# Block 1's expert weights read in whole rows, with the order of the gate and up products changed to fit

## The reference, cut to what matters

```
hidden = silu(x @ w_gate[e]) * (x @ w_up[e])
y      = hidden @ w_down[e]
lat[tokens of e] += g2 * affinity * y
```

## Time and profile before

| what | value |
|---|---|
| time, median of 3 runs | 2313.15 us (2310.91 to 2315.34) |
| the profiled execution's own time | 2319.69 us |
| its span | 2318.0 us |
| TensorE matmuls busy | 2019.3 us, 87% |
| DVE busy | 1720.3 us, 74% |
| ACT busy | 1246.9 us, 54% |
| mean rate of the DMA engines | 275 GB/s |

### The profile page before, as it was taken

The page is one execution under the profiler, slowest core; times in us unless marked ns, Lnnn a source line. Parts: engine busy times, 40 slices in busy tenths (PEclk is TensorE's granted clock), DMA queues, the critical chain, the costliest instruction groups (busy, mean ns, idle before and its releaser), DMA issues.

```text
span 2318.0 us, 30942 instructions
## 1 busy us (share of the span) xinstructions
PE 2019.3 (87%) x9479; PEld 1669.3 (72%) x9479; DVE 1720.3 (74%) x1894; ACT 1246.9 (54%) x1464; POOL 309.1 (13%) x313
## 2 busy tenths in 40 slices
PE   3999999837999999999598888944999999999980
PEld 2888878636888877877476777843888888888760
DVE  5676665398999999998534544443999999999877
ACT  2311112206888878777524412213888888888763
POOL 1000001100100011110301540113010001000023
PEclk9999999858999999999798999966999999999995
DMA  9276863607999999999711113344999999999986
GB/s 314 81 248 223 265 217 110 244 10 276 382 380 388 382 379 389 383 380 349 276 38 55 31 36 117 118 172 141 400 412 411 411 412 412 411 411 412 377 312 231
DMA packets 241520, 637.19 MB, mean 275 GB/s; under 512 B 20340, under 2 KB 57480, under 8 KB 241452
## 3 DMA queue, kind: packets, MB, share of 16 engines
q1 hardware_dynamic: 209536, 524.35, 60.3%
q0 software_dynamic: 27680, 97.70, 12.0%
q10 hardware_dynamic: 4236, 14.27, 1.6%
HBM read 575.83 MB, written 60.41 MB: 274 GB/s over the span
## 4 chain that ended last, share of the span: by engine, by line
PE 65%; DVE 12%; DMA 9%; issue 5%; SPq 4%; ACT 3%; POOL 1%; ACTq 0%; DVEq 0%; POOLq 0%; PEldq 0%
PE ps L1962 19%; PE ps L1963 19%; PE ps L1965 19%; DMA ring<-in_moe_w_down 5%; SPq L522 4%; PE ps L2370 1%; DVE mL L1469 1%; DMA h_dram<-h2t 1%; DMA ring<-in_ada_w 1%; PE ps L2085 1%; DVE top_i L1452 1%; DVE top_v L1451 1%; DVE affT L1454 1%; DVE xz L1615 1%; PE ps L2220 1%
## 5 line engine op out<-in xcount | busy, mean ns | idle before, releaser
L1839 DVE TENSOR_TENSOR mL<-ring,mH 128x1024 fp32r<-128x1024 f32 x384 | 454.7, 1221 | 37.8 <-ACT mH L1166 34.0
L1469 DVE TENSOR_TENSOR mL<-ring,mH 128x1024 fp32r<-128x1024 f32 x384 | 455.4, 1221 | 31.7 <-ACT mH L994 22.4
L994 ACT ACTIVATE mH<-ring 128x1024 fp32r<-128x1024 f32 x384 | 401.6, 1062 | 97.7 <-PE ps L1965 62.8
L1962 PE MATMUL ps<-mH,xsH 128*128 128x512 f32 x1088 | 437.4, 402 | 7.4 <-DVE mL L1839 4.4
L1965 PE MATMUL ps<-mH,xsL 128*128 128x512 f32 x1088 | 426.9, 392 | 0.0
L1963 PE MATMUL ps<-mL,xsH 128*128 128x512 f32 x1088 | 426.7, 392 | 0.0
L1166 ACT ACTIVATE mH<-ring 128x1024 fp32r<-128x1024 f32 x384 | 390.9, 1054 | 31.9 <-PE ps L1965 31.9
L1962 PEld LDWEIGHTS ps<-mH,xsH 128*128 128x128 f32 x1088 | 205.9, 189 | 48.8 <-issue 7.3
L1965 PEld LDWEIGHTS ps<-mH,xsL 128*128 128x128 f32 x1088 | 205.6, 189 | 45.2
L1963 PEld LDWEIGHTS ps<-mL,xsH 128*128 128x128 f32 x1088 | 206.0, 189 | 39.6
L1962 PE MATMUL ps<-mH,hidH 128*128 128x512 f32 x544 | 216.8, 399 | 13.0 <-DVE hidL L1514 5.8
(11 more groups left out here) (402 smaller groups left out, 3030.9 us busy)
## 6 DMA issues: line engine op xcount, KB each, us to landing
ring<-in_w_expert_gate SPq DMA_DIRECT2D x144, 512.0 KB
ring<-in_w_expert_up SPq DMA_DIRECT2D x144, 512.0 KB
ring<-in_w_expert_down SPq DMA_DIRECT2D x144, 512.0 KB
ring<-in_moe_w_gate SPq DMA_DIRECT2D x128, 512.0 KB
ring<-in_moe_w_up SPq DMA_DIRECT2D x128, 512.0 KB
ring<-in_moe_w_down SPq DMA_DIRECT2D x128, 512.0 KB
ring<-in_ada_w SPq DMA_DIRECT2D x96, 512.0 KB
yslot_dram<-xz POOLq DMA_DIRECT2D x31, 512.0 KB, 7.0
```

Source lines behind the costliest of these rows:

```text
L994: act.activation(mH[:, m % WSETS, :], ring[:, m % RING, :], ACT.Copy).then_inc(S["m1_hi"], 1)
L1469: dve.tensor_tensor(mL[:, m % WSETS, :], ring[:, m % RING, :], mH[:, m % WSETS, :].bitcast(F32), ALU.subtract).then_inc(S["m1_lo"], 1)
L1839: dve.tensor_tensor(mL[:, wset, :], ring[:, slot, :], mH[:, wset, :].bitcast(F32), ALU.subtract).then_inc(S["m2_lo"], 1)
L1962: pe.matmul(o, high, rh, start=start, stop=False)
```

## The change

Chunks 0 to 7 become gate, 8 to 15 up, each one k with all 1024 columns, as down already was. TensorE multiplies each chunk for both halves of the columns, except the last three of up (LATE = 3): chunks 13, 14 and 15 are first multiplied for the first half, then `m1_up_half` is raised, and then for the second half, each raising `m1_used` as it ends. ACT takes one SiLU of both halves at m = 13. DVE multiplies half 0 at m = 19 and half 1 at m = 20; ACT copies the transposed halves at m = 21 and 22, DVE subtracts at m = 20 and 22. TensorE makes all transposes behind chunk 15: first half, next expert's tokens, second half.

```diff
@@ -19,6 +19,7 @@
 RING = 12
 SPLIT_RING = 6
 ADA_RING = 4
+LATE = 3
 WSETS = 6
 E1 = 16
 CAP1 = 2 * T // E1
@@ -30,7 +31,7 @@
     h2_done x1_done var2 rstd2 h2_out y_ready zs_hi tr2 h2T_ready sq2 zs_lo
     rt_done wait_passed ada_done split_done z_done m1_lo hy_done pool_out unused_zero m2_y final_done consts
     masks var_ready rstd_ready stored m1_tok m1_y_done zero_row tok_zero rows_zero rows_in small_in
-    silu_ready sq_done mod_ready tr_ready tr_hi split_hi f_part cv_done c_copied route1 e1_exp m1_used m1_hi
+    silu_ready sq_done mod_ready tr_ready tr_hi split_hi f_part cv_done c_copied route1 e1_exp m1_used m1_up_half m1_hi
     m1_xT m1_xT_hi slots_ready m1_silu m1_hT m1_hT_hi if_zero gate_in if_hi v_even gate_exp branch d2_out uc_ready 
     q_mm pm_ready pv hn_tr num_out final_in dve_steps cols_tr mod_mm xn_done
     tr_lo sums_out sums2_out sums_in row_cols row_tr row_copied rows_out rows_here c_here mid_tr tr_mid v_mm pool_steps neg_out mb_in mask_done exp_done small_ready small_exp sq_out intra_out kt_mm kw_out st_mm c_ready hd_out cell_w ov_l last_y last_out row_one aff_ready affT_tr m1_xT_lo m1_hid m1_hT_lo if_lo v_odd if_mm pool_mm k_mm k_out s_mm
@@ -255,7 +256,7 @@
         [("m1_xT", 2 * E1), ("m2_xT", 2 * (E2 + 1 + NOVF))],
         [("m1_xT_hi", 2 * E1), ("m2_xT_hi", 2 * (E2 + 1 + NOVF))],
         [("m1_xT_lo", 2 * E1), ("m2_xT_lo", 2 * (E2 + 1 + NOVF))],
-        [("m1_silu", 2 * E1), ("m2_silu", E2), ("ov_silu", NOVF)],
+        [("m1_silu", E1), ("m2_silu", E2), ("ov_silu", NOVF)],
         [("m1_hid", 2 * E1), ("m2_hid", E2), ("ov_hid", 2 * NOVF)],
         [("m1_hT", 2 * E1), ("m2_hT", E2), ("ov_hT", 2 * NOVF)],
         [("m1_hT_hi", 2 * E1), ("m2_hT_hi", E2), ("ov_h", 2 * NOVF)],
@@ -513,13 +514,7 @@
                     sp.wait_ge(S["m1_lo"], 24 * e + c - RING + 1)
                     if not static(q):
                         settle(sp)
-                if c < 16:
-                    n, kp = c // 8, (c % 8) // 2
-                    src = (moe_g, moe_u)[c % 2][e, :, 2 * kp:2 * kp + 2, 512 * n:512 * n + 512]
-                    dst = ring[:, s, :].rearrange("p (k n) -> p k n", k=2)
-                else:
-                    src, dst = moe_d[e, :, c - 16, :], ring[:, s, :]
-                sp.dma_start(dst, src).then_inc(ring_in[s], 16)
+                sp.dma_start(ring[:, s, :], (moe_g, moe_u, moe_d)[c // 8][e, :, c % 8, :]).then_inc(ring_in[s], 16)
 
         in_pairs(sp, E1, m1_step)
 
@@ -1006,12 +1001,12 @@
         def m1_step(q, r):
             e = 2 * q + r
             for m in range(24):
-                if m == 13 or m == 21:
-                    n = m // 21
-                    act.wait_ge(S["m1_used"], 24 * e + 8 * n + 8)
-                    act.activation(sg[:, 512 * n:512 * n + 512], ps[:, n, :], ACT.Silu).then_inc(S["m1_silu"], 1)
-                if m == 19 or m == 23:
-                    j = m // 23
+                if m == 13:
+                    act.wait_ge(S["m1_used"], 24 * e + 8)
+                    act.activation(sg.rearrange("p (a b) -> p a b", a=2), ps[:, 0:2, :],
+                                   ACT.Silu).then_inc(S["m1_silu"], 1)
+                if m == 21 or m == 22:
+                    j = m - 21
                     act.wait_ge(S["m1_hT"], 2 * e + j + 1)
                     act.activation(hidH[:, 4 * j:4 * j + 4, :].rearrange("p a b -> p (a b)"), ps[:, 2 * j, :],
                                    ACT.Copy).then_inc(S["m1_hT_hi"], 1)
@@ -1502,13 +1497,17 @@
                     tokens(e + 1, 1 - r, 0)
                 if m == 6 and not (static(q) and e == 0):
                     y_out(q, 0) if r == 1 else y_out(q - 1, 1)
-                if m == 13 or m == 21:
-                    n = m // 21
-                    dve.wait_ge(S["m1_silu"], 2 * e + n + 1)
+                if m == 19 or m == 20:
+                    n = m - 19
+                    if n == 0:
+                        dve.wait_ge(S["m1_silu"], e + 1)
+                        dve.wait_ge(S["m1_up_half"], e + 1)
+                    else:
+                        dve.wait_ge(S["m1_used"], 24 * e + 16)
                     dve.tensor_tensor(hid[:, 512 * n:512 * n + 512], sg[:, 512 * n:512 * n + 512], ps[:, 2 + n, :],
                                       ALU.mult).then_inc(S["m1_hid"], 1)
-                if m == 19 or m == 23:
-                    j = m // 23
+                if m == 20 or m == 22:
+                    j = m // 22
                     dve.wait_ge(S["m1_hT_hi"], 2 * e + j + 1)
                     part = hidH[:, 4 * j:4 * j + 4, :].rearrange("p a b -> p (a b)")
                     dve.tensor_tensor(hidL[:, 4 * j:4 * j + 4, :].rearrange("p a b -> p (a b)"), ps[:, 2 * j, :],
@@ -2129,20 +2128,29 @@
             e = 2 * q + r
             first = static(q) and e == 0
             pe.wait_ge(S["m1_xT_lo"], 2 * e + 2)
+
+            def rows_part(m, halves):
+                k, w = m % 8, [slice(512 * n, 512 * n + 512) for n in halves]
+                return three([ps[:, 2 * (m // 8) + n, :] for n in halves], xsH[:, r, k, :], xsL[:, r, k, :],
+                             [(mH[:, m % WSETS, at], mL[:, m % WSETS, at]) for at in w], k == 0, k == KD - 1)
+
             for m in range(24):
-                pe.wait_ge(S["m1_lo"], 24 * e + m + 1)
                 if m < 16:
-                    n, kp, u = m // 8, (m % 8) // 2, m % 2
-                    bank = ps[:, n + 2 * u, :]
-                    if m % 8 == 0 and not first:
-                        pe.wait_ge(S["m1_hid"], 2 * e + n - 1)
+                    if m == 0 and not first:
+                        pe.wait_ge(S["m1_hid"], 2 * e)
                         pe.wait_ge(S["m1_hT_lo"], 2 * e)
-                    for k2 in range(2):
-                        k = 2 * kp + k2
-                        w = slice(512 * k2, 512 * k2 + 512)
-                        last = three([bank], xsH[:, r, k, :], xsL[:, r, k, :],
-                                     [(mH[:, m % WSETS, w], mL[:, m % WSETS, w])], k == 0, k == KD - 1)
+                    if m < 16 - LATE:
+                        pe.wait_ge(S["m1_lo"], 24 * e + m + 1)
+                        last = rows_part(m, (0, 1))
+                    else:
+                        if m == 16 - LATE:
+                            for m0 in range(m, 16):
+                                pe.wait_ge(S["m1_lo"], 24 * e + m0 + 1)
+                                last = rows_part(m0, (0,))
+                            last.then_inc(S["m1_up_half"], 1)
+                        last = rows_part(m, (1,))
                 else:
+                    pe.wait_ge(S["m1_lo"], 24 * e + m + 1)
                     k = m - 16
                     if k == 0 and not first:
                         pe.wait_ge(S["m1_y_done"], e)
@@ -2152,12 +2160,10 @@
                                  [(mH[:, m % WSETS, 512 * n:512 * n + 512], mL[:, m % WSETS, 512 * n:512 * n + 512])
                                   for n in range(2)], k == 0, k == KD - 1)
                 last.then_inc(S["m1_used"], 1)
-                if m == 13:
+                if m == 15:
                     h_transposes(e, 0)
-                if m == 15:
                     if not (static(q) and e == E1 - 1):
                         x_transposes(e + 1, 1 - r, 16 * q + (16 if r == 0 else 32))
-                if m == 17:
                     h_transposes(e, 1)
 
         in_pairs(pe, E1, m1_step)
```

## The result

The changed kernel takes 2320.72 us (median of 7 runs, 2318.37 to 2322.7), the kernel before 2313.11 us (7 runs). The ratio is 1.0029 with a 95% interval of 1.0019 to 1.0038: slower by 6.7 us, 4.4 to 8.8 (the two medians themselves are 7.6 us apart). In a second measurement both kernels were 5 to 8 us slower than in the first, and the ratio between them was 1.0014 (1.0006 to 1.0023). The forecast was +4.5 us, a ratio of 1.0019: in both intervals, in the first at its lower end. The forecast time was 2317.6 us with a range of 2308 to 2323; 2320.72 us is in the range and 3.1 us above the forecast, beyond the 2316 to 2319.5 given for the likeliest case.

What follows compares the result with a forecast made beforehand. Block 1's expert stage was taken as TensorE-bound for seven periods, then supply-bound. Better supply -8.4 us and the new order +12.9 us sum to +4.5 us on 2313.15: 2317.6 us, range 2308 to 2323.

Steps and rivals of the forecast that it cites:

- the likeliest case: Walk and sum right within 1.5 us, chance 0.58 including rival C's time; 2316 to 2319.5 us.
- the 8.4 us: Block 1's expert stage: all that better weight supply can give, 562.6 us against 554.2 for TensorE alone.
- the last piece: End of block 1's expert stage, 1053.52 to 1100.56: 47.0 us against 46.1 of TensorE work, 0.9 us lost.
- The walk: One expert's end of up, step by step from the last up matmul's slot end: +0.75 us per expert.
- the first stop: TensorE idle before the second half's transposes, waiting for DVE's second multiply: 0.76 us.
- The 12.9 us: Cost of the new product order: 0.75 us for each of 15 experts, 1.6 us for the last.
- What is late next: Second half's hidL, done at 5.7 to 6.4, wanted before the fifth down chunk at 7.9: that wait goes.
- Rival C: Supply no better in 4 KB runs, yet hardly binding in the new order: still +4.5, 2317.6 us; chance within 0.58.
- Rivals A: End of up: DVE's second multiply finishes under TensorE's transposes, all 8.4 us kept: 2304.7 us, chance 0.13.
- B: End of up: wait half hidden, 0.35 us per expert: -2.8, 2310 us; chance 0.16, shared with A and C together.
- D: Second stop per expert near the fifth down chunk or in split chunks: 2324 to 2329 us, chance 0.13.
- The sign: Whole kernel's direction against about 0.2%, 4.6 us, of resolution: faster 0.13, same 0.45, slower 0.42.

Runs made afterwards that it cites:

- rows_only: Kernel before, its own product order, gate and up loaded as whole 4 KB rows (column pairing wrong): stage 553.8 us, whole time 2327.93 us in one run.
- moved: Changed kernel with hidden-value transposes behind chunk 14 and the first down chunk, DVE and ACT steps reordered to suit: 0.9983 of before, stage 557.8 us.
- moved_2kb: Kernel moved with gate and up rows written in two 2 KB pieces: 1.0017 of before, stage 566.3 us.
- dve_first: Changed kernel with DVE's second multiply and first hidL ahead of the split of chunk 19: 0.9991 of before, stage 561.8 us.
- after_2kb: Changed kernel with gate and up rows written in two 2 KB pieces, TensorE's slices swapped to match: stage 566.0 us.

## Why the prediction was right

*What bounds the stage before, and the 8.4 us.* Right, and now shown: the long runs alone took 8.8 us from the first profile's stage (10.0 from the second's) and left the period at TensorE's 34.52. One count was wrong and its number right: the last piece of the kernel before, from 1053.52, holds three groups of four transposes (at 1057.13, 1085.82 and 1091.76), not two; the 46.1 us given for it is 46.05 in rows_only.

*The walk.* Each step against the rows above, in us from the last up slot's end: split of chunk 19 -0.07 forecast and -0.07 measured, second multiply 1.06 and 1.07, hidL 1.66 and 1.67, transposes behind the multiply 1.90 and 1.81, first down product 2.50 and 2.50. The miss of 0.09 is that TensorE followed this DVE result by 0.06 us, where I had taken the 0.15 seen behind hidL; and the eight transposes between ended at 1.23, not 1.14. So the first stop is 0.58 us and not 0.76, and the second 0.34 and not 0.25. Neither changed the sum, as hidL came last anyway. The 12.9 us of the walk are 13.0 to 13.3 against rows_only. The period was forecast at 35.2 to 35.4 and is 35.27; the stage was forecast at 562.6 + 4.5 = 567.1 and is 567.1. That it agrees to the last digit is luck: a second profile of the kernel before has 563.8, and over the two profiles of each kernel the difference is 3.0 to 4.4 us.

*What is late next.* Right: hidL of the second half ended at 6.42 (forecast 6.4), the fifth down chunk began without a stop, and ACT's waits for landed chunks ended.

*Rival C.* Its claim about the rate is false (rows_only, and moved beside moved_2kb), its arithmetic right: with short runs the changed order took 566.0 us. So the result would have been the same whether the supply got better or not.

*Rivals A, B and D.* None happened in the changed kernel. Of the kernels with another order, B's -2.8 us lies between what dve_first (-0.8 in the stage, against the first profile) and moved (-4.8) came to.

*What was off.* The sign I had left open between "same" (0.45) and "slower" (0.42), with the larger chance on what did not come: both intervals lie above 1. The first measurement has 6.7 us, of which the stage's profiles show 4.4. The other 2.3 us are in no piece of the four profiles that repeats; the second measurement has 3.3 us. Both intervals allow 4.4, the first only at its edge. I can't say more than that from one profiled execution each. And I had expected the DMA share to fall under 1.0; it is 1.01 and 1.02 at 384 and 386 GB/s, 1.02 and 1.03 in rows_only at 393 and 396, where TensorE waits for nothing, and 1.04 and 1.05 in after_2kb, where it waits for no weights either. The share didn't tell a queue that is the limit from one that isn't; the step in the period and the waits for landed chunks did.

## What to carry to other kernels

When an order of work is turned to suit the loads, list what each in-order engine has in front of the instructions that close the gap, and when each of those can start: here a split whose buffer was freed late stood before a multiply that was ready, and moving the ready ones in front of it gave back 5 of 13 us. A supply limit that shows only after seven experts is worth just the difference to the next limit, and a change that raises that next limit above it gets nothing from the better supply. Where two effects of opposite sign are each two to three times their sum, one at a time in a stage read from the trace tells more than the whole time does.

## What the runs showed of the hardware that I had not expected

- Moving from 2 KB to 4 KB runs raised the delivered rate from 387 to about 410 GB/s in slices without an adding write.
- A DMA share of 1.05 stood both where chunks came late and held TensorE up (before, 383 GB/s) and where they did not (after_2kb, 383 GB/s); with long runs it was 1.02 and 1.03 and nothing waited (rows_only, 393 and 396 GB/s).
- TensorE's first transpose started 0.06 us after a DVE multiply written to `xz`, its first down product 0.15 us after the end of a DVE subtraction to hidL.
- The same unchanged code outside the stage took up to 6 us more or less between profiled executions (the part after block 2's experts: 142.7, 146.7, 147.8 and 148.5 us).
